# Running maxima of all prompt chunks at once, decay factors with keys on the partitions, and attention scores as three products of rounded halves

## The reference, cut to what matters

```python
b = jnp.cumsum(lf, axis=-1)
dmat = jnp.where(causal, b[..., :, None] - b[..., None, :] + li[..., None, :], -jnp.inf)
inter = b + m0[..., None]
m = jnp.maximum(inter, jnp.max(dmat, axis=-1))
dexp = jnp.exp(dmat - m[..., None])
iscale = jnp.exp(inter - m)
s = jnp.einsum('bhtd,bhsd->bhts', qs, k) * dexp
num = iscale[..., None] * jnp.einsum('bhtd,bhdv->bhtv', qs, C0) + jnp.einsum('bhts,bhsv->bhtv', s, v)
den = iscale * jnp.einsum('bhtd,bhd->bht', qs, n0) + jnp.sum(s, axis=-1)
h = num / jnp.maximum(jnp.abs(den), jnp.exp(-m))[..., None]
m_new = m[..., -1]
w = jnp.exp(b[..., -1:] - b + li - m_new[..., None])
```

## Time and profile before

| | |
|---|---|
| median of 3 runs | 2996.79 us (2996.43 to 2997.97) |
| profiled execution, own time | 2997.7 us |
| its span | 2995.9 us |
| TensorE matmul busy | 2918.8 us, 97% of the span |
| weight load / VectorE / ScalarE / GpSimd busy | 93% / 60% / 46% / 22% |
| mean granted TensorE clock | 0.986 of full speed |
| DMA | 419.71 MB, mean 140 GB/s |

### The profile page before, as it was taken

The page is one execution under the profiler, slowest core; times in us unless marked ns, Lnnn a source line. Parts: engine busy times, 40 slices in busy tenths (PEclk is TensorE's granted clock), DMA queues, the critical chain, the costliest instruction groups (busy, mean ns, idle before and its releaser), DMA issues.

```text
span 2995.9 us, 43868 instructions
## 1 busy us (share of the span) xinstructions
PE 2918.8 (97%) x16347; PEld 2777.6 (93%) x16347; DVE 1786.6 (60%) x2655; ACT 1392.4 (46%) x2445; POOL 648.0 (22%) x939
## 2 busy tenths in 40 slices
PE   8999999999999998999999999999999999999997
PEld 7888789888888887999999999999999999999997
DVE  4222247766767655655477764777547775477654
ACT  3222225554555444554355553555535545355443
POOL 1111011111111111221123221232212322134222
PEclk9999989999999998999999999999999999999998
DMA  5342355545554444443434545345443454334433
GB/s 164 124 142 94 98 176 165 173 139 187 187 173 150 137 138 142 138 153 116 153 114 139 155 141 160 113 138 157 143 153 112 143 160 140 121 113 123 132 119 79
DMA packets 245925, 419.71 MB, mean 140 GB/s; under 512 B 38610, under 2 KB 161874, under 8 KB 245714
## 3 DMA queue, kind: packets, MB, share of 16 engines
q1 hardware_dynamic: 243602, 416.77, 44.5%
q10 hardware_dynamic: 2112, 0.13, 0.0%
HBM read 352.12 MB, written 65.74 MB: 139 GB/s over the span
## 4 chain that ended last, share of the span: by engine, by line
PE 61%; DVE 1%; DMA 1%; issue 1%; ACT 1%; SPq 0%; POOL 0%; DVEq 0%; ACTq 0%; POOLq 0%
PE f_ps L1754 41%; PE f_ps L1759 20%; DMA f_sgi<-gate_rows 0%; PE f_st L1766 0%; DVE f_rinv L1972 0%; DMA both_high<-gate_rows 0%; DMA both_high<-in_w_out 0%; ACT f_wh L1816 0%; DVE f_ml L1967 0%; DVE both_low L1976 0%; ACT f_mh L1846 0%; ACT L1825 0%; DVE f_wl L1951 0%; SPq L1689 0%; POOL f_sgi L2113 0%
## 5 line engine op out<-in xcount | busy, mean ns | idle before, releaser
L1951 DVE TENSOR_TENSOR f_wl<-both_high,f_wh 128x1024 fp32r<-128x1024 f32 (+2 forms) x460 | 542.9, 1180 | 140.8 <-ACT f_wh L1816 135.3
L1754 PE MATMUL f_ps<-f_xh,f_wh 128*128 128x416 f32 x1760 | 618.9, 352 | 3.2 <-DVE f_xl L1985 3.2
L1754 PE MATMUL f_ps<-f_xl,f_wh 128*128 128x416 f32 x1760 | 619.2, 352 | 0.0
L1816 ACT ACTIVATE f_wh<-both_high 128x1024 fp32r<-128x1024 f32 (+2 forms) x460 | 442.1, 964 | 281.7 <-PE f_ps L1759 276.9
L1759 PE MATMUL f_ps<-f_xh,f_wl 128*128 128x416 f32 x1760 | 367.9, 351 | 0.0
L1754 PEld LDWEIGHTS f_ps<-f_xh,f_wh 128*128 128x128 f32 x1760 | 330.4, 188 | 11.3 <-DVE f_xl L1985 4.1
L1754 PEld LDWEIGHTS f_ps<-f_xl,f_wh 128*128 128x128 f32 x1760 | 331.4, 188 | 4.0 <-issue 0.6
L1759 PEld LDWEIGHTS f_ps<-f_xh,f_wl 128*128 128x128 f32 x1760 | 329.9, 188 | 2.3
L2004 DVE SCALAR_TENSOR_TENSOR both_high<-both_high,f_taps 128x416 f32<-128x416 f32 (+2 forms) x264 | 154.3, 598 | 296.6 <-ACT both_high L1868 296.4
L1754 PE MATMUL f_ps<-f_gh,f_wh 128*128 128x416 f32 x880 | 310.9, 353 | 5.9 <-issue 5.9
L701 PE MATMUL pp<-gxh,gwh 128*128 128x416 f32 x800 | 302.3, 378 | 12.3 <-DVE gxl L673 12.3
(11 more groups left out here) (251 smaller groups left out, 5123.1 us busy)
## 6 DMA issues: line engine op xcount, KB each, us to landing
both_high<-in_w_up SPq DMA_DIRECT2D x220, 512.0 KB, 3.7
both_high<-in_w_dn SPq DMA_DIRECT2D x120, 384.0 KB, 3.1
both_low<-in_w_gate SPq DMA_DIRECT2D x80, 512.0 KB, 4.0
both_high<-in_w_br SPq DMA_DIRECT2D x40, 512.0 KB, 3.9
both_high<-in_w_out SPq DMA_DIRECT2D x40, 512.0 KB, 3.6
gate_rows<-gsgo SPq DMA_DIRECT2D x98, 208.0 KB, 2.9
f_sgi<-gate_rows SPq DMA_DIRECT2D x52, 208.0 KB, 4.0
proj_rows<-both_high SPq DMA_DIRECT2D x12, 900.0 KB, 4.5
```

The costliest lines, as they stand in the source:

```text
L1754: pe.matmul(ps[n][:, 0:TB], wh[s][:, (col + k) * P:(col + k) * P + P], x[:, k0 + k, :], start=(k == 0 and x is xhi), stop=False)
L1816: act.activation(wh[v % WS][:, 0:w], raw[s][:, 0:w], ACT.Copy).then_inc(ev("w_hi"), 1)
L1951: dve.tensor_tensor(wl[n][:, 0:w], raw[s][:, 0:w], wh[n][:, 0:w].bitcast(F32), ALU.subtract).then_inc(ev("w_lo"), 1)
```

## The change

1. The running maxima of all 16 prompt chunks are computed once, during the sample chunk: a is transposed to 64 rows (16 chunks x 4 heads) of 128 tokens, a doubling scan of 7 maxima runs along it, and the result is transposed back. The last column of each chunk is broadcast by two small matmuls, the 16 states m0 are chained by 32 small VectorE instructions, and one exponential over 256 columns gives all factors (iscale, exp(-m), w, decay). The 16 rows of -M go to HBM, and each chunk loads its own, broadcast over the partitions (256 KB a chunk).
2. The decay of a prompt chunk is built with keys on the partitions: the loaded row, plus a transposed mask, exponential with bias a. The q k products are taken with keys as rows, so their decayed form is already what `mix_pe_intra` needs. `mix_pe_a`, `mix_pe_last`, `mix_pe_str` and the VectorE and ScalarE work that goes with them stay in the sample chunk alone.
3. The scores of prompt chunks are three fp32r products of rounded halves instead of one float32 product; the halves come from the ScalarE copy that was there (now rounding) and two VectorE subtractions.
4. `SLOTS` becomes (1, 3, 1, 1, 2, 1, 2), with the same 11 halves in one place less.

The core of the diff (the new one-time pieces are named `run_*`):

```diff
-SLOTS = (1, 2, 1, 1, 1, 2, 1, 2)
+SLOTS = (1, 3, 1, 1, 2, 1, 2)
@@ SP, at the start of chunk n for chunk n + 1
+        def maxima_load(n):
+            wait(sp, "sb_ready", n - 2 if n > S + 1 else S)
+            sp.dma_start(decays[q][:].rearrange("p h t -> p (h t)"), mxs[row_of(n)].partition_broadcast(P)
+                         ).then_inc(ev(f"mr_in{q}"), 16)
@@ SP, sample chunk, after slot 3
+                sp.wait_ge(ev("nmt_ready"), 1)
+                sp.dma_start(mxs.rearrange("n (h t) -> (n h) t", h=MH), run[0][0:4 * CHUNKS, 0:P]).then_inc(ev("mxs_out"), 16)
+                sp.wait_ge(ev("mxs_out"), 16)
+                maxima_load(S + 1)
@@
+    def run_pe_back(pe):
+        pe.wait_ge(ev("run_max"), 7)
+        wait(pe, "am_ready", S)
+        pe.transpose(p3[:, 0:W4], run[1][0:W4, P // 2:P // 2 + P], K("ident", W4)[:, 0:W4]).then_inc(ev("cmx_tr"), 1)
+    def run_pe_last(pe):
+        pe.wait_ge(ev("cmx_ready"), 1)
+        pe.matmul(p3[:, W4:2 * W4], K("last"), flat(cmx[:]), start=True, stop=True)
+        pe.matmul(p3[:, 2 * W4:3 * W4], K("last"), flat(ball[:, 0:CHUNKS, :]), start=True, stop=True).then_inc(ev("lastv_done"), 1)
+    def run_dve_max(dve):
+        for i in range(7):
+            src, dst, at = run[i % 2][0:W4], run[1 - i % 2][0:W4], P // 2
+            wait(dve, "run_max", i)
+            dve.tensor_tensor(dst[:, at:at + P], src[:, at:at + P], src[:, at - 2 ** i:at + P - 2 ** i], ALU.max
+                              ).then_inc(ev("run_max"), 1)
+    def run_dve_states(dve):
+        for c in range(CHUNKS):
+            wait(dve, "m0_step", c)
+            dve.tensor_tensor(mlall[:, c, :], m0all[:, c, :], lastv[:, 0, c, :], ALU.max).then_inc(ev("ml_step"), 1)
+            dve.wait_ge(ev("ml_step"), c + 1)
+            dve.tensor_tensor(m0all[:, c + 1, :], mlall[:, c, :], lastv[:, 1, c, :], ALU.add).then_inc(ev("m0_step"), 1)
@@ def mix_pe_scores(pe, n, q, i)
         for jj in range(2):
-            for g in range(KVH):
-                mm = pe.matmul(p45[:, g, ...], aqt[r:r + HD, 2 * i + jj, :], ktr[r:r + HD, :, :], start=True, stop=True)
+            for x, y in ((aqt, ktr), (aqt, ktl), (aql, ktr)):
+                for g in range(KVH):
+                    mm = pe.matmul(p45[:, g, ...], x[r:r + HD, 2 * i + jj, :], y[r:r + HD, :, :],
+                                   start=(y is ktr and x is aqt), stop=(x is aql))
@@
+    def mix_dve_mask(dve, n, q):
+        dve.wait_ge(ev(f"mr_in{q}"), 16 * ((n - S + 1) // 2))
+        dve.tensor_tensor(decays[q][:], decays[q][:], bc(K("mask_t")[:, None, :], [P, MH, P]), ALU.add
+                          ).then_inc(ev("masked"), 1)
+    def mix_dve_low(dve, n, q):
+        wait(dve, "aqt_ready", n)
+        dve.tensor_tensor(aql[:], p45[:, 1, :].rearrange("p (a b) -> p a b", a=4), aqt[:].bitcast(F32), ALU.subtract)
+        wait(dve, "kt_ready", n)
+        dve.tensor_tensor(ktl[:, q, :], P_KT, ktr[:, q, :].bitcast(F32), ALU.subtract)
+    def mix_act_decay(act, n, q):
+        wait(act, "masked", n - S)
+        for h in range(MH):
+            ins = act.activation(decays[q][:, h, :], decays[q][:, h, :], ACT.Exp, bias=acall[:, row_of(n), h:h + 1])
@@ TensorE, prompt chunk
             mix_pe_scores(pe, n, q, 0)
             mix_pe_s(pe, n, q)
-            mix_pe_a(pe, n, q)
             units_pe(pe, n, 0)
             mix_pe_scores(pe, n, q, 1)
             units_pe(pe, n, 1)
-            mix_pe_last(pe, n, q)
-            units_pe(pe, n, 2)
             mix_pe_ptr(pe, n, q, 0)
-            mix_pe_str(pe, n, q)
             mix_pe_inter(pe, n, q)
@@ VectorE, prompt chunk: now
             mix_dve_sm(dve, n, q, 0); mix_dve_s(dve, n, q); units_dve(dve, n, 0)
             mix_dve_sm(dve, n, q, 1); mix_dve_pn(dve, n, q, 0); units_dve(dve, n, 1)
             mix_dve_inter(dve, n, q); mix_dve_pn(dve, n, q, 1); units_dve(dve, n, 2)
...
             mix_dve_h2(dve, n, q); mix_dve_mask(dve, n + 1, 1 - q); mix_dve_h3(dve, n, q); units_dve(dve, n, 5)
             mix_dve_low(dve, n + 1, 1 - q); units_dve(dve, n, 6)
```

More of the change, by code:

```diff
@@ L47, in constants @@
     parts["tri_s"] = causal.T & same
-    parts["mask"] = np.where(causal, 0.0, NEG)
+    parts["mask_t"] = np.where(causal.T, 0.0, NEG)
     parts["mask_s"] = np.where(causal & same, 0.0, NEG)
@@ L392, in mixer_phase @@
     xns, prs, hhs, sgs = scratch["normed"], scratch["rows"], scratch["mixed"], scratch["gates"]
+    mxs = scratch["maxima"]
     low, high = scratch["low"], scratch["high"]
@@ L423, in mixer_phase @@
     rm, nmx = sb("rm", [P, 4]), sb("nmx", [P, 4])
+    run = [sb(f"run{i}", [P, P // 2 + P]) for i in range(2)]
+    cmx, lastv = sb("cmx", [P, CHUNKS, 4]), sb("lastv", [P, 2, CHUNKS, 4])
+    m0all, mlall = sb("m0all", [P, CHUNKS + 1, 4]), sb("mlall", [P, CHUNKS, 4])
+    exall = sb("exall", [P, 4, CHUNKS, 4])
+    nmall = lastv[:, 0]
+    decall = sb("decall", [P, CHUNKS, 2])
     m0 = sb("m0", [P, 4])
@@ L772, in mix_pe_tr @@
         wait(pe, "hat_ready", 2 * n - 2)
-        wait(pe, "m_ready", n)
+        wait(pe, "m_ready", min(n, S + 1))
         if n == S + 1:
@@ new lines, in run_pe_last, with run_pe_out, run_dve_rows @@
+    def run_pe_last(pe):
+        pe.wait_ge(ev("cmx_ready"), 1)
+        pe.matmul(p3[:, W4:2 * W4], K("last"), flat(cmx[:]), start=True, stop=True)
+        pe.matmul(p3[:, 2 * W4:3 * W4], K("last"), flat(ball[:, 0:CHUNKS, :]), start=True, stop=True).then_inc(ev("lastv_done"), 1)
+    def run_pe_out(pe):
+        pe.wait_ge(ev("nmall_ready"), 1)
+        wait(pe, "st_ready", S)
+        pe.transpose(p3[0:W4, 0:P], flat(nmall), K("ident")).then_inc(ev("nmt_tr"), 1)
+    def run_dve_rows(dve):
+        dve.wait_ge(ev("run_tr"), 1)
+        dve.memset(run[0][:, 0:P // 2], NEG)
+        dve.memset(run[1][:, 0:P // 2], NEG)
+        dve.tensor_copy(run[0][0:W4, P // 2:P // 2 + P], p3[0:W4, P:2 * P]).then_inc(ev("run_ready"), 1)
@@ L781, in mix_pe_a, with run_act_out @@
+    def run_act_out(act):
+        act.wait_ge(ev("nmt_tr"), 1)
+        act.activation(run[0][0:W4, 0:P], p3[0:W4, 0:P], ACT.Copy).then_inc(ev("nmt_ready"), 1)
     def mix_pe_a(pe, n, q):
+        pe.wait_ge(ev("run_ready"), 1)
         wait(pe, "adiag_ready", n)
@@ L793, in mix_pe_s @@
             r = DK * (h % 2)
-            mm = pe.matmul(p67[:, h % 2, P * (h // 2):P * (h // 2) + P], qkt[r:r + DK, h // 2, :],
-                           qkt[r:r + DK, 2 + h // 2, :], start=True, stop=True)
+            rows, cols = (h // 2, 2 + h // 2) if n == S else (2 + h // 2, h // 2)
+            mm = pe.matmul(p67[:, h % 2, P * (h // 2):P * (h // 2) + P], qkt[r:r + DK, rows, :],
+                           qkt[r:r + DK, cols, :], start=True, stop=True)
         mm.then_inc(ev("s_done"), 1)
@@ L809, in mix_pe_scores @@
             wait(pe, "qkt_ready", n)
+            wait(pe, "aql_ready", n - 1)
+            wait(pe, "ktl_ready", n - 1)
         else:
@@ L835, in mix_pe_intra @@
     def mix_pe_intra(pe, n, q):
-        wait(pe, "st_ready", n)
+        rows = st if n == S else sbuf
+        wait(pe, "st_ready", min(n, S))
         wait(pe, "inr_ready", n)
         for h in range(MH):
-            mm = pe.matmul(p67[:, h % 2, DA * (h // 2):DA * (h // 2) + DA], st[:, h, :], va[q][:, h, :],
+            mm = pe.matmul(p67[:, h % 2, DA * (h // 2):DA * (h // 2) + DA], rows[:, h, :], va[q][:, h, :],
                            start=True, stop=True)
@@ L868, in mix_pe_pv @@
         wait(pe, "vr_ready", n)
-        wait(pe, "m_ready", n + 1)
+        wait(pe, "m_ready", S + 1)
         wait(pe, "hat_ready", 2 * n - 2 + i)
@@ L879, in mix_pe_hm @@
         wait(pe, "hm_ready", n)
-        wait(pe, "st_ready", n)
+        wait(pe, "st_ready", S)
+        wait(pe, "nmt_ready", 1)
+        wait(pe, "hmt_ready", n - 1)
         for h in range(MH):
@@ L891, in mix_dve_a, with mix_dve_max @@
                           ).then_inc(ev("adiag_ready"), 1)
-    def mix_dve_max(dve, n, q, mask="mask"):
+    def mix_dve_max(dve, n, q, mask="mask_s"):
         wait(dve, "a_done", n)
@@ L914, in mix_dve_s @@
         wait(dve, "dx_ready", n)
-        wait(dve, "s_tr", n - 1)
+        wait(dve, "s_tr", min(n - 1, S))
+        wait(dve, "intra_done", n - 1)
+        dx = decays[q if n > S else 1]
         for e in range(2):
@@ L1121, in samp_pe_scores @@
             r = HD * g
-            pe.matmul(p45[:, g, P:P + SAMP], aqp[r:r + HD, :], ktr[r:r + HD, 0, 0:SAMP], start=True, stop=True)
+            pe.matmul(p45[:, g, P:P + SAMP], aqp[r:r + HD, :], kts[r:r + HD, 0:SAMP], start=True, stop=True)
         for b in range(SEQS):
@@ L1284, in _ @@
         units_pe(pe, S, 0)
+        run_pe_back(pe)
         mix_pe_last(pe, S, 0, "last_s")
@@ L1287, in _ @@
         units_pe(pe, S, 1)
+        run_pe_last(pe)
         mix_pe_str(pe, S, 0)
@@ L1294, in _ @@
         units_pe(pe, S, 3)
+        run_pe_out(pe)
         samp_pe_pv(pe)
@@ L1429, in _ @@
         samp_act_pt(act)
+        run_act_all(act)
         units_act(act, S, 3)
+        run_act_out(act)
```

162 lines of the change are left out of this document (108 added, 54 removed).

## The result

The changed kernel takes 2977.16 us (median of 4 runs, 2973.72 to 2979.13) against 2997.38 us (2996.43 to 2999.77) for the kernel before on the same chip: a ratio of 0.993, 95% interval 0.9918 to 0.9941. That is 20.2 us less, where 31.1 were forecast; the time lies inside the range given. The profiled execution took 2978.5 us, with a span of 2976.7 us against 2995.9, so 19.2 us less.

What follows compares the result with a forecast made beforehand. TensorE's queue was taken to bound the prompt chunks, waits part of the sample chunk. Gains 25.8 + 8.3 + 2.0 less 5.0 made 31.1 us, from 2996.8 to 2965.7, say 2966; range 2955 to 2986.

Steps and rivals of the forecast that it cites:

- fourth rival: Prompt chunks: a new wait of 1 us for probabilities or normed rows in each of 16, 2982 us; chance 0.13.
- fifth: Prompt chunks: what is removed was not the bound, VectorE's chain or the weights are, 2993 to 2997 us; chance 0.03.
- first case: Whole kernel: the forecast itself, 31.1 us gained, 2966 us, own range 2955 to about 2978; chance 0.73.
- second rival: Prompt chunks' scores: pairs don't run side by side, 1.43 us a call, 8.1 us gained, 2989 us; chance 0.07.
- third: Prompt chunks' scores: weight loads laid bare, 1.86 us a call instead of 0.97, 3002 us; chance 0.04.
- pieces that leave, 16 chunks: Prompt chunks: broadcast of a 0.86, last-row broadcast 0.23, four transposes 0.52 us leave TensorE; 25.8 us gained.
- scores, 32 calls: Prompt chunks' scores: six fp32r pairs take 0.71 us instead of 0.97, 0.26 gained a call, 8.3 us in all.
- stalls in prompt chunks: Where spans begin: chunk 7 gains 0.5 us, chunk 14 loses its 1.45 us wait; 2.0 us gained together.
- sample chunk: Sample chunk: added scan wait, transposes, small matmuls and a later state update cost 5.0 us, bounds 2 and 9.
- 3 us more: Prompt chunks' scores: bound if the 0.10 us lateness behind a float32 piece vanishes, 32 x 0.10 gained besides.
- The wait itself: Sample chunk behind slot 0: TensorE waits 2.9 us for VectorE's scan of seven maxima.
- 9 if TensorE comes out of the wait at the low clock: Sample chunk: upper cost bound, 9 us, with about 3 us for low clock and the update waiting 2.

Runs made afterwards that it cites:

- The filled wait: Changed kernel with three unread 512-column float32 matmuls on TensorE ahead of the transpose of the scan's result; 2971.9 us, ratio 0.9912.
- The four repairs: Changed kernel with scan's result behind samples' scores, exponential later, span turn ahead of first exponentials, gating moved to chunk 13; 2965.26 us, ratio 0.9893.
- this part alone: Kernel before with only the three fp32r score products and the two VectorE subtractions put in; 2991.53 us, ratio 0.998.

## Why the prediction was right, and where it was off

**Right: the bound and the mechanism.** TensorE's queue sets the prompt chunks; the broadcast put back costs 0.87 us in a plain chunk, where it was priced at 0.86. The case forecast is the one that came, the rates of the new call are close to those assumed, and no wait appeared in the plain chunks (fourth rival), nor did the time stay (fifth). The total was less well hit than the case: 2977.2 lies 1 us inside the slow end of the range of the first case (2978), which had been built from a sample chunk of 9 and scores without gain. The first came true, the scores fell short by 3.2 of 8.3, and terms that no bound held made up the rest. That it fell inside is in part luck. A call takes 0.81 us, so the second rival's 1.4 us and the third's 1.9 are out. On the third: the loads of L932 last 0.19 us like those of the earlier trace rows, consecutive pairs lie on the same rows, and still they start 0.12 apart; so for 64 rows too the load of a pair lies beside the pair ahead. The Trainium skill ("TensorE: Matmul & The Clock Gate", Part 3), by which a load overlaps only when its row group differs, isn't borne out by this trace.

**Off: 11.9 us of gain**, by the profiled executions. Term by term, forecast against trace:

| term | forecast | trace | short by |
|---|---|---|---|
| pieces that leave, 16 chunks | 25.8 | 16 x 1.51 = 24.2 | 1.6 |
| scores, 32 calls | 8.3 | 32 x 0.16 = 5.1 | 3.2 |
| stalls in prompt chunks | 2.0 | 0.5 (rest of 29.8) | 1.5 |
| sample chunk | -5.0 | -9.0 | 4.0 |
| untouched parts | 0 | -1.6 | 1.6 |

*The pieces.* 0.52 for the transposes L832 was their distance in the timeline. The prediction counted for L784 and L802 how late the matmul behind them is; here it didn't ask whether the piece behind L832 was late for another reason and would stay late. It would: 0.09 remain, 16 times. The reason is the one of the next paragraph: L824 and L941 are the first pieces over 64 rows behind pieces over 128.

*The scores.* "Six pairs at 0.119 take 0.71" forgot that the first of a place costs more: it takes 0.22. The prediction had read this lateness for matmuls behind float32 pieces, and credited none for an fp32r pair over 64 rows behind unit matmuls over 128. 32 x 0.10 is the whole of the missing 3.2. It was in the old call too: there the pairs start at 612.95, 613.27, 613.49 and 613.70, so the first takes 0.32 and the others 0.21, and the 0.97 that the new call was compared with holds the same 0.10. And it is the shape that makes it, not the data type. The weight loads of four places in the changed kernel show it, beside their matmuls, which start at 614.09, 614.90, 625.73 and 626.70:
```profile
614.08 0.19 PEld L932 LDWEIGHTS p<-ktr,aqt 64*128 64x128 f32 x2 [0.28 <-issue]
...
614.78 0.54 PEld L906 LDWEIGHTS p<-qkt 64*128 64x128 f32 x8
...
625.55 0.98 PEld L980 LDWEIGHTS p<-cst,sm 128*128 128x128 f32 x8
626.70 0.52 PEld L941 LDWEIGHTS p<-cst,qkt 64*128 64x128 f32 x8 [0.17 <-issue]
```
Where the shape stays (L906 behind the scores, 64 rows both; L980 behind a unit, 128 rows both), the first load runs 0.12 and 0.18 us ahead of its matmul, beside the last of the piece before, and nothing is late. Where it changes (the scores behind a unit, L941 behind L980), the first load starts with its matmul: the scores start 0.09 late and their second pair another 0.10. So it is at every change of tile shape, rows or columns, in the plain chunk of either kernel (0.09 ahead, 0.05 to 0.11 behind), with float32 or fp32r on either side. Float32 pieces of the unit matmuls' own shape leave a lateness too (0.09 behind L802, 0.40 behind L784), but that one is not in the scores. The bound of "3 us more", for a lateness that was to go with float32, could not come (behind a scores call the first unit matmul takes 0.30 now and took 0.29 before).

*Where a span begins.* In chunk 7 0.64 us was gained (0.5 forecast). In chunk 14 the 1.45 was to go as a whole; 0.80 of it stayed, and the products with V, which now come sooner, wait 1.42 for ScalarE's copy of the probabilities, where 0.38 was lost before. The chunk gained 1.45 us where a plain one gains 1.84, so 0.4 was lost instead of 1.5 gained. The step at fault is that I asked what VectorE does sooner and not what stands next behind it. In chunk 13 a wait of 1.28 came that wasn't in any list: VectorE's masked scores stand behind its wait for ScalarE at the gating, and had 0.86 us in hand before. The gain in every second chunk (0.1 each, 0.9 in chunk 3) stands against these two.

*The sample chunk.* The wait itself was forecast at 2.9 and measured 2.65; the last rows at 0.8 and measured 1.07 with their place. What was off: "9 if TensorE comes out of the wait at the low clock" stood as a bound and was what happened. The rows for it were at hand: behind 4.56 us of waiting in chunk 7 the clock was low, behind 1.45 in chunk 14 it wasn't. 2.9 lies between, and the sample chunk's stretch had a mean clock of 0.88 already. Taking the full clock was a choice without a row. The filled wait shows what it cost, some 3 us of the 4.0. The price in the bound, "about 3 us", fits, though not by its reading: behind the 4.56 us it was one half of 12 matmuls that ran at 0.35 us, some 2 us more than at full clock, and not three places. Another 1.4 us of waiting, for the gates (L758), is scatter that no term could have held. The update of the states waited 1.74 instead of the forecast 1 in this profile (0.51 in the next), from ScalarE's queue as argued; the run with the later exponential shows the cause, not its size.

The four repairs were worth 12.0 us together; alone 4.3 (scan result), 2 to 3 (exponential, not sharp) and 5.6 (span turn), and the gating nothing.

**Open.** What a scores call would cost if its pairs did not run side by side; what decides whether the clock falls behind a wait (it did behind 2.65 and 3.89 us, not behind 0.80, 1.28 and 1.42), and why it falls at the states' matmuls without one; what the wait for the scan costs without the clock. The transposes and the last-row broadcast that left (0.66 us a chunk) were read from the timelines and not put back in a run.

## What to carry to other kernels

In a stage that TensorE bounds, price a piece by the distance to the second matmul behind it, and count the changes of tile shape before and after: each cost 0.14 to 0.20 us here (0.09 ahead of its first matmul, 0.05 to 0.11 behind it), for float32 and fp32r pieces alike, so it stays when a piece is replaced by one of the same shape. Left out on one side of the comparison, it was 3.2 of the 8.3 us forecast for the scores. When a wait is added to TensorE, look up whether waits of that length in the same trace were followed by the low clock, and put the low clock into the forecast, not only into the range; often an independent piece can be moved into the gap, and even unread work in it pays. Shortening a chunk uncovers waits that had no row before, most of all in the chunks that do something once (a new span, a gating), so go through those one by one.

## What the runs showed that was not expected

Matmuls on different row halves ran in pairs though the program issued three of one half and then three of the other: if the queue holds them as the program gives them, the partner came from three places further on, at the cost of nothing (0.12 us from pair to pair).

Three unread float32 matmuls of 512 columns inside a wait kept the granted clock at 1.00 (2.4 GHz) instead of 0.62 over 9 us and made the sample chunk some 3 us shorter. After 2.65 us without work the clock was low, and 32 records that take 2.03 us took 3.77; behind the waits of 0.80, 1.28 and 1.42 us in chunks 13 and 14 it stayed at 1.00. And around the states' matmuls (32 rows each) it fell to the lower level in every kernel: 0.51 over 9 us in the kernel before and with the exponential later, 0.50 from 446 to 455 us in the changed one, waits or not.

A pair of matmuls of 256 columns over 64 rows takes 0.118 us, while the first of a call takes 0.22, in the changed kernel and in the kernel before with this part alone. Such an extra (0.05 to 0.11), and another 0.09 ahead of the first matmul, stands at every change of tile shape of a plain chunk, where the weight load starts with the matmul instead of ahead of it.
